# Routing by tiles, gate sums around the combination, and products of constants in two gaps of a hybrid decoder block

## The reference

```python
h = modulate(rms_norm(x, g_ffn[layer]), sh_f, sc_f)
g_logits = ht @ w_group + b_group
gate_group = softmax(g_logits)[g_sel]           # g_sel: the best group
e_logits = (ht @ w_erouter[g_sel]) + b_expert   # 8 experts of that group
top_vals, top_idx = lax.top_k(e_logits, 2)
top_w = jax.nn.softmax(top_vals, axis=-1)
...
out += (silu(ht @ w1[e]) * (ht @ w3[e]) * combine) @ w2[e]
x = x + gt_f * out
```

## Time and profile before

| | us |
|---|---|
| median of three runs | 626.9 |
| the profiled execution | 627.78 |
| its span | 625.8 |
| TensorE busy | 546.5 (87%) |
| VectorE busy | 294.6 (47%) |
| ScalarE busy | 184.0 (29%) |
| GpSimd busy | 79.0 (13%) |

### The profile page before, as it was taken

How to read it: one execution, slowest core, us unless ns; L and a number is a source line. 1 busy time by engine, 2 the same in 40 slices (tenths; PEclk the granted TensorE clock), 3 DMA queues, 4 the chain that set the end, 5 groups by cost and what they waited for, 6 DMA issues and landing times.

```text
span 625.8 us, 7694 instructions
## 1 busy us (share of the span) xinstructions
PE 546.5 (87%) x2982; PEld 343.9 (55%) x2982; DVE 294.6 (47%) x497; ACT 184.0 (29%) x328; POOL 79.0 (13%) x100
## 2 busy tenths in 40 slices
PE   1499999999978999999999747899999889879797
PEld 1377768778766676665446414445555444434443
DVE  4978673376798636562032284323322222312216
ACT  5265462344444457882042211000000000000002
POOL 8131100000010000000031111111221111110000
PEclk9999999999998999999999958999999999989999
DMA  8986855595262064001930485999999999999957
GB/s 336 398 262 232 308 193 205 172 366 202 68 214 90 2 264 206 1 1 51 426 128 34 186 339 177 407 417 421 422 420 419 419 421 420 421 420 420 410 233 293
DMA packets 42626, 169.28 MB, mean 271 GB/s; under 512 B 7848, under 2 KB 9896, under 8 KB 30308
## 3 DMA queue, kind: packets, MB, share of 16 engines
q1 hardware_dynamic: 32356, 140.81, 56.3%
q0 software_dynamic: 9104, 25.95, 11.8%
q10 hardware_dynamic: 1136, 2.11, 0.9%
HBM read 160.74 MB, written 16.25 MB: 283 GB/s over the span
## 4 chain that ended last, share of the span: by engine, by line
PE 61%; DVE 13%; DMA 13%; SPq 7%; ACT 4%; issue 2%; POOL 0%; DVEq 0%; ACTq 0%; POOLq 0%
PE banks L1784 11%; PE banks L1675 9%; PE banks L1804 5%; DMA qkT<-in_w_dram 5%; DMA obuf<-in_w_dram 4%; PE banks L1627 4%; PE banks L1510 4%; PE banks L1512 4%; PE banks L1511 4%; DVE mixT L893 3%; PE banks L1611 2%; DMA qkT<-in_w_ada_dram 2%; PE banks L1504 2%; PE banks L1502 2%; PE banks L1503 2%
## 5 line engine op out<-in xcount | busy, mean ns | idle before, releaser
L1804 PE MATMUL banks<-stage,work 128*64 128x512 f32 x168 | 60.1, 610 | 6.4 <-ACT work L855 6.4
L853 ACT ACTIVATE work<-banks 128x256 f32<-128x256 f32 x16 | 6.1, 383 | 200.3 <-PE banks L1784 200.3
L1784 PE MATMUL banks<-qkT,work 128*64 128x256 f32 x272 | 62.4, 386 | 0.0
L1675 PE MATMUL banks<-stage,mixT 128*128 128x512 f32 x128 | 56.2, 595 | 0.0
L1324 DVE TENSOR_TENSOR work<-banks,gates 128x1024 f32<-128x1024 f32 x15 | 18.4, 1225 | 74.5 <-PE banks L1804 74.5
L1318 DVE TENSOR_TENSOR work<-work,banks 128x256 f32<-128x256 f32 x16 | 6.7, 421 | 87.6 <-ACT work L853 87.6
L1784 PE MATMUL banks<-hT,work 128*64 128x256 f32 x192 | 44.0, 387 | 2.5 <-DMA qkT<-in_w_dram 2.5
L1512 PE MATMUL banks<-hT_hi,w_lo 128*128 128x512 f32 x112 | 43.8, 391 | 0.0
L893 DVE SCALAR_TENSOR_TENSOR mixT<-stage,small,mixT 128x1024 f32<-128x1024 f32 x32 | 41.0, 1282 | 0.7
L1510 PE MATMUL banks<-hT_hi,w_hi 128*128 128x512 f32 x96 | 40.4, 421 | 0.0
L1675 PEld LDWEIGHTS banks<-stage,mixT 128*128 128x128 f32 x128 | 24.1, 191 | 28.8 <-issue 28.8
(11 more groups left out here) (301 smaller groups left out, 1172.6 us busy)
## 6 DMA issues: line engine op xcount, KB each, us to landing
stage<-in_w_dram SPq DMA_DIRECT2D x31, 1024.0 KB
qkT<-in_w_dram SPq DMA_DIRECT2D x23, 1024.0 KB
stage<-in_w_ada_dram POOLq DMA_DIRECT2D x16, 1024.0 KB, 5.7
hT<-in_w_dram SPq DMA_DIRECT2D x12, 1024.0 KB
stage<-in_w_in_dram SPq DMA_DIRECT2D x5, 2048.0 KB, 11.0
val<-in_w_dram SPq DMA_DIRECT2D x10, 1024.0 KB
mixT<-in_w_dram SPq DMA_DIRECT2D x10, 1024.0 KB
alibi<-in_w_dram SPq DMA_DIRECT2D x5, 1024.0 KB
```

The costliest lines, as they stand in the source:

```text
L1675: ins = mm(banks[:, w % 5, :], mixT[:, k, t * P:(t + 1) * P], wv[:, k % 4, half * 512:(half + 1) * 512], start=(k == 0), stop=(k == KD - 1))
L1784: ins = mm(banks[half * C:(half + 1) * C, 2, up * F:(up + 1) * F], heT[:, r, k * P + half * C:k * P + (half + 1) * C], ws[2 * place + half ...
L1804: ins = mm(banks[half * C:(half + 1) * C, 4 + 2 * r + col, :], geT[:, fc * P + half * C:fc * P + (half + 1) * C], w2s[2 * place + half][:, ...
```

## The change

- `add_shift` waits for the tile's logits and for `r2_ready`, which ScalarE gives after the reciprocal root. ScalarE squares the last tile before it evicts x2T.
- The selection is put into functions on a range of tiles. Tiles 0 and 1 are done between the output halves 6 and 7, tile 2 around the copy of x2T, tile 3 after the last logits. The rank products are ordered by the tile they need. TensorE waits for `logits_read` before it writes logits of the tiles 2 and 3 into the bank that VectorE reads.
- Counts, column and slot are rounded by adding and subtracting 1.5 * 2^23 times the step. The table holds a key (1024 minus the token) and a second product of four passes says which choice it was; the rows to gather come from one instruction, the rows to scatter from two more. The scan for the plan moves behind the tables.
- `ADA_STEPS` goes from (0, 2, 4, 6, 8, 9, 10, 11) to (0, 2, 4, 6, 8, 10, 11, 12); from the fifth quarter on its first half stands before the combination, the second behind it and behind the splitting of weights. The first half of the second gate moves from step 12 to 13.
- Products of constants: 16 after the fourth and 12 after the seventh sum of the scale vector in the head, of 256 columns; 4 of 512 columns between the first two sets of transposes of experts' rows. TensorE waits for `scatter_ready` before the first of these.

```diff
-ADA_STEPS = (0, 2, 4, 6, 8, 9, 10, 11)
+ADA_STEPS = (0, 2, 4, 6, 8, 10, 11, 12)
+FILLERS_BETWEEN = 4
+HEAD_FILLERS = ((KD // 2, 16), (KD - 1, 12))
+TO_C, TO_P = 1.5 * 2.0 ** 23 * C, 1.5 * 2.0 ** 23 * P
...
-    steps[12].append((("gate", 1, 0), None))
+    steps[13].append((("gate", 1, 0), None))
...
             for t in range(NT):
+                act.wait_ge(x2_ready, 2 * t + 2)
+                a.activation(obuf[:, 2:4, :].rearrange("p a b -> p (a b)"), xr[:, t, :], ACT.Square,
+                             accum_out=ss2[:, t:t + 1]).then_inc(ss2_ready, 1)
                 if t == NT - 1:
...
-                link(a.activation(r2[:, t:t + 1], r2[:, t:t + 1], ACT.Exp, scale=-0.5))
+                a.activation(r2[:, t:t + 1], r2[:, t:t + 1], ACT.Exp, scale=-0.5).then_inc(r2_ready, 1)
+                act.wait_ge(r2_ready, t + 1)
...
                 if s in ADA_STEPS:
                     i = ADA_STEPS.index(s)
-                    ada_quarter(SCALE_F + i // 4, i % 4)
-                    if s < NT * DH:
-                        combine_unit(s)
+                    ada_open(SCALE_F + i // 4, i % 4)
+                    if i < 4:
+                        ada_close(SCALE_F + i // 4, i % 4)
+                    combine_unit(s)
...
                 for n in split_at(s):
                     w_rest(n)
+                if s in ADA_STEPS[4:]:
+                    i = ADA_STEPS.index(s)
+                    ada_close(SCALE_F + i // 4, i % 4)
...
+                if w == 2 * NT - 2:
+                    dve.wait_ge(memset_ready, 7)
+                    dve.wait_ge(logits_done, 2)
+                    link(v.tensor_copy(common, banks[:, 5, NT * NR:(NT + 1) * NR]))
+                    add_shift(0)
+                    add_shift(1).then_inc(logits_read, 1)
+                    dve.wait_ge(logits_read, 1)
+                    best_of_each(0, 2)
+                    second_of_each(0, 2)
+                    link(group_masks(0, 2))
...
+            add_shift(NT - 2).then_inc(logits_read, 1)
+            dve.wait_ge(logits_read, 2)
+            best_of_each(NT - 2, NT - 1)
             dve.wait_ge(fT_done, NT)
             dve.wait_ge(logits_done, NT - 2)
             v.tensor_copy(x2T[:, (NT - 1) % 2, 0:512], banks[:, 6, :]).then_inc(x2T_ready, 1)
+            second_of_each(NT - 2, NT - 1)
+            link(group_masks(NT - 2, NT - 1))
...
+            best_of_each(NT - 1, NT)
+            second_of_each(NT - 1, NT)
+            link(group_masks(NT - 1, NT))
+            link(v.memset(extra[:, 0:1], 0.0))
...
-            link(v.tensor_scalar(ints[:, 0:32], banks[:, 0, n32:n32 + 32], float(C - 1), None, ALU.add))
-            link(v.tensor_scalar(ints[:, 0:32], ints[:, 0:32], C.bit_length() - 1, None, ALU.arith_shift_right))
-            link(v.tensor_scalar(extra, ints[:, 0:32], -1.0, 0.0, ALU.add, ALU.max))
-            link(v.tensor_tensor_scan(incl, extra, zero32, 0.0, ALU.add, ALU.add))
-            link(v.tensor_tensor(obase, incl, extra, ALU.subtract))
-
-            link(v.scalar_tensor_tensor(out=obase, in0=obase, scalar=float(C), in1=over_base, op0=ALU.mult, op1=ALU.add))
+            link(v.tensor_scalar(extra[:, 1:E + 1], counts, -(C // 2 + 0.5), TO_C, ALU.add, ALU.add))
+            link(v.tensor_scalar(extra[:, 1:E + 1], extra[:, 1:E + 1], -TO_C, 0.0, ALU.add, ALU.max))
+            link(v.tensor_tensor_scan(obase, extra[:, 0:E], over_step, 0.0, ALU.add, ALU.add))
...
-            link(v.tensor_copy(posi, posf))
-            v.tensor_scalar(hi_i, posi, 4096 - P, None, ALU.bitwise_and)
-            link(v.tensor_scalar(lo_i, posi, P - 1, None, ALU.bitwise_and))
-            v.tensor_copy(rt[:, 1480:1488], lo_i)
-            link(v.tensor_copy(rt[:, 1488:1496], hi_i))
+            link(v.tensor_scalar(hi_big, posf, -(P // 2 - 0.5), TO_P, ALU.add, ALU.add))
+            link(v.scalar_tensor_tensor(out=lo_neg, in0=hi_big, scalar=TO_P, in1=posf, op0=ALU.subtract, op1=ALU.subtract))
...
-            link(v.tensor_scalar(free, held, 0.0, float(SKIP), ALU.is_equal, ALU.mult))
-            link(v.scalar_tensor_tensor(out=found, in0=held, scalar=-1.0, in1=free, op0=ALU.add, op1=ALU.add))
-            link(v.tensor_scalar(free, found, float(T), float(-T), ALU.is_ge, ALU.mult))
-            v.tensor_tensor(tables[:, 0, :], found, free, ALU.add).then_inc(table_ready, 1)
-            v.tensor_copy(tables[:, 1, :], found).then_inc(scatter_ready, 1)
+            v.tensor_scalar(tables[:, 0, :], held, -1.0, float(2 * T), ALU.mult, ALU.add).then_inc(table_ready, 1)
+            link(v.tensor_scalar(pair_row, held, -1.0, float(2 * T), ALU.mult, ALU.add))
+            v.scalar_tensor_tensor(out=tables[:, 1, :], in0=second_choice, scalar=float(T), in1=pair_row,
+                                   op0=ALU.mult, op1=ALU.add).then_inc(scatter_ready, 1)
...
+                    for rows_summed, count in HEAD_FILLERS:
+                        pe.wait_ge(scale_used, rows_summed)
+                        for n in range(count):
+                            mm(banks[:, 0, 256:512], ones_bf[:], ones_bf[:].unsqueeze(1).to_broadcast([P, 2, P]),
+                               start=False, stop=True, skip_group_check=True)
...
             logits(NT - 2)
             rows_T(NT - 1)
+            pe.wait_ge(y_scaled, 2 * NT)
+            pe.wait_ge(masks_ready, 1)
+            ranks_of(0)
+            ranks_of(1)
             logits(NT - 1)
+            pe.wait_ge(masks_ready, 2)
+            ranks_of(2)
+            pe.wait_ge(masks_ready, 3)
+            ranks_of(3).then_inc(rank_done, 1)
...
+            pe.wait_ge(scatter_ready, 1)
             expert_T(None, rows_of(0), 0)
+            for n in range(FILLERS_BETWEEN):
+                mm(banks[:, 7, :], ones_bf[:], ones_bf[:].unsqueeze(1).to_broadcast([P, NT, P]), start=True, stop=True)
             expert_T(None, rows_of(1), 1, 6)
```

More of the change, by code:

```diff
@@ L292, in hymba_block @@
             "xnb_ready", "xn_stored", "fT_done", "x2T_ready", "logits_done"))
+        ss2_ready, r2_ready, logits_read = sem("ss2_ready"), sem("r2_ready"), sem("logits_read")
         wrA_ready, x2T_act, scatter_ready = sem("wrA_ready"), sem("x2T_act"), sem("scatter_ready")
@@ L935, in ada_quarter, with ada_close @@
                 link(accumulate(acc[:, vec % 2, :], src[:, 0, :], 2 * i, i == 0))
+            def ada_close(vec, i):
+                n, src, _, _ = quarter(vec, i)
                 if i == 3 and vec in (SHIFT_F, SCALE_F):
@@ L1193, in _, with best_of_each @@
-            dve.wait_ge(logits_done, NT - 1)
-            link(v.tensor_copy(common, banks[:, 5, NT * NR:(NT + 1) * NR]))
-            dve.wait_ge(xnb_ready, NT - 1)
-            for t in range(NT - 1):
-                ins = add_shift(t)
-            link(ins)
+            def best_of_each(a, b):
+                r = slice(a * (G + 1), b * (G + 1))
+                n = (b - a) * (G + 1)
+                link(v.tensor_reduce(top1[:, r], lg[:, r, :], X, ALU.max))
+                link(v.tensor_tensor(first[:, r, :], lg[:, r, :], spread_rows(top1[:, r], n), ALU.is_equal))
+                link(v.tensor_tensor(first[:, r, :], first[:, r, :], rev.unsqueeze(1).to_broadcast([P, n, EG]), ALU.mult))
+                link(v.tensor_reduce(key1[:, r], first[:, r, :], X, ALU.max))
+                link(v.tensor_tensor(hot1[:, r, :], first[:, r, :], spread_rows(key1[:, r], n), ALU.is_equal))
@@ new lines, in second_of_each @@
+            def second_of_each(a, b):
+                r = slice(a * G, b * G)
+                n = (b - a) * G
+                link(v.scalar_tensor_tensor(out=rest.rearrange("p (t g) j -> p t (g j)", t=NT)[:, a:b, :],
+                                            in0=experts(hot1)[:, a:b, :], scalar=-1e30,
+                                            in1=experts(lg)[:, a:b, :], op0=ALU.mult, op1=ALU.add))
+                link(v.tensor_reduce(top2[:, r], rest[:, r, :], X, ALU.max))
+                link(v.tensor_tensor(second[:, r, :], rest[:, r, :], spread_rows(top2[:, r], n), ALU.is_equal))
+                link(v.tensor_tensor(second[:, r, :], second[:, r, :], rev.unsqueeze(1).to_broadcast([P, n, EG]), ALU.mult))
+                link(v.tensor_reduce(key2[:, r], second[:, r, :], X, ALU.max))
+                link(v.tensor_tensor(hot2[:, r, :], second[:, r, :], spread_rows(key2[:, r], n), ALU.is_equal))
@@ new lines, in of_group, with group_masks @@
+            def of_group(k, src, a, b):
+                return v.tensor_tensor(masks[:, k, a:b, :].rearrange("p t (g j) -> p t g j", g=G),
+                                       src[:, a:b, :].rearrange("p t (g j) -> p t g j", g=G),
+                                       gsel[:, a:b, :].unsqueeze(3).to_broadcast([P, b - a, G, EG]), ALU.mult)
+            def group_masks(a, b):
+                link(v.tensor_tensor(hots_t[:, a:b, :], hot2_t[:, a:b, :], experts(hot1)[:, a:b, :], ALU.add))
+                of_group(2, hots_t, a, b).then_inc(masks_ready, 1)
+                of_group(0, experts(hot1), a, b)
```

(25 more changed lines are left out.)

130 lines of the change are left out of this document (54 added, 76 removed).

## The result

The changed kernel takes **619.6 us** (median of 4, 618.37 to 620.81) against 626.28 for the kernel before on the same chip (4 runs): 0.9891 of it, with an interval of 0.9868 to 0.9914. It is faster by 6.7 us where 9.0 were forecast (617.9). The profiled execution took 618.37, its span is 616.4. The two spans shown, 625.8 and 616.4, lie 9.4 apart, but the first belongs to a slower execution of its kernel and the second to the fastest of its own. I go by the medians for what the change is worth, and by both pairs of traces for where it comes from.

The account below looks back on a forecast made before the run. The last 26 experts' weights were taken as a stream of fixed length (200 us) starting after the first `h1_done`. Head 0.9, gate sums 3.0 and routing 5.1 sum to 9.0: 626.9 - 9.0 = 617.9 us, range 615.4 to 622.2.

Parts of the forecast that it names:

- head: Scale vector's sums: 28 products of constants lift TensorE's clock, so ScalarE's evictions start sooner; 0.9 us, bound 1.0.
- gate sums: Attention steps 8 to 11: fewer VectorE sums ahead of the combinations shorten TensorE's waits; 3.0 us, ceiling 6.4.
- routing: From the last half of x2 to the first `h1_done`: earlier gather and kept clock bring it forward by 5.1 us.
- gather sooner: Routing: the table is ready 4.0 us sooner, so the gather starts 3.6 to 4.0 earlier; 3.8 taken.
- gather slowed by weights: The earlier gather meets weights still filling the DMA engines; 0 to 2 us lost, 0.7 taken, as gathered rows are few.
- clock kept between the transposes: First experts: four products hold TensorE at 2.4 GHz, turning rows 3.1 us earlier into `h1_done` 5.3 earlier, 5.1 taken.
- 9 sooner: Sign for the last experts' weight stream: its first weights issued and its last landing 9 us sooner.
- A: Rival: clock falls between the two transposes as before and the gather pays 2 us; 621.7 us, chance 0.16.
- B: Rival: attention gains 5.0 instead of 3.0, gather undisturbed, no doubt about the clock left; 615.0 us, chance 0.07.
- D: Rival: TensorE's waits in attention step 9 drop its clock to the end of step 12; 631.5 us, chance 0.03.
- C: Rival: routing and head leave nothing at the end, attention 2.0; 624.9 us, no measurable change, chance 0.05.
- E: Rival: rounding by addition gives another table, adding one expert pair to the stream; 633.2 us, chance 0.01.

Follow-up runs that it names:

- run 2: The kernel before with only the 28 products of constants in the head added: 625.02 us, ratio 0.9976 to the kernel before.
- run 1: The changed kernel without the 28 products of constants in the head: 621.94 us, ratio 0.9943 to the kernel before.
- run 3: The changed kernel with the gate sums as before (steps 8 to 11, both halves ahead of the combination): 622.47 us, ratio 0.9950 to the kernel before.
- run 5: The kernel before with head, gate sums and products between the transposes changed, but the old routing: 622.67 us, ratio 0.9942 to the kernel before.
- run 7: The changed kernel with w3 of the sixth expert issued only once the second gathered rows have landed: 616.57 us, ratio 0.9842 to the kernel before.
- run 4: The changed kernel without the four products of constants between the two sets of transposes: 619.87 us, ratio 0.9904 to the kernel before.
- run 6: The changed kernel and the kernel before, both unaltered, profiled again as the second pair of traces: 619.11 us and 626.77 us.
- run 10: The changed kernel with w3 of the sixth expert held back and without the four products between the transposes: 616.47 us, ratio 0.9840 to the kernel before.
- run 9: The kernel before with w3 of the sixth expert held back until the second gathered rows have landed: 625.62 us, ratio 0.9988.

## Why the prediction was nearly right, and where it failed

The time fell into the range (615.4 to 622.2), and the sign and the mechanism held: three gains add up to one earlier start of a stream of fixed length. The sum was 9.0 against 6.7 measured; the time missed by 1.7 only, since the sum was taken from 626.9 and the kernel before came to 626.28 beside the changed one. Term by term:

| term | counted | shown | by |
|---|---|---|---|
| head | 0.9 | 1.4 | run 2 and the trace of run 1; evictions 1.09 sooner |
| gate sums | 3.0 | 2.9 | run 3 |
| routing, of this: | 5.1 | 3.1 | run 5 |
| gather sooner | 3.8 | 4.4 | 20.5 to 16.1 after x2, in 12 of 13 traces |
| gather slowed by weights | -0.7 | -1.5 to -2.5 | 5.96 to 7.02, mean 6.4, against 4.51 to 4.67, mean 4.6; run 7 |
| clock kept between the transposes | 2.0 (2.2 less 0.2 for doubt) | about 0 | runs 4, 5, 6, 10 |

The three shown come to 7.4 by medians, within their errors of the 6.7. By the ratios to the kernel before, gate sums and routing would be 3.7 and 3.2, with an error of some 1.8 each; only the traces are finer than that. They give the routing less: from the last half of x2 to the first `h1_done` there are 31.7 to 32.4 in four traces of the old routing (33.8 in the one shown before), 29.1 to 31.4 in five of the new one, and 27.1 to 27.3 in the three with a weight held back. The means are 32.2, 30.2 and 27.2, so the routing gives 2.1, and 5.0 once its gather runs alone; with 1.4 and 2.8 the change comes to 6.3. Of the 3.0 between 30.2 and 27.2 the gather's rows are 2.1. Another 0.7 lies behind the first transposes: TensorE waits 1.8 to 2.7 for the late rows, and in three of the five traces its clock was down after that wait, in none of the three with a weight held back.

**Head: right**, a little more than its bound of 1.0. The bound followed ScalarE's evictions; TensorE's own transposes, which stand ahead of the projections, were at the lower clock too and gained the rest. All signs named for it were there, 1.95 for the sums of columns and 35.72 for the evictions (35.8 was forecast).

**Gate sums: right in size, and by its main argument**, that VectorE's work ahead of the combinations sets the time. The 1.6 that it added for the clock, "4.8 + 1.6 = 6.4", is not a second price: it is the wait that a faster TensorE has instead (run 2, 6.4 of waiting at the full clock). The waits for the combination are 2.6 and not under 2 as forecast, and there are the 1.3 for the bank, of which the prediction said that the product waits "as long as before". The time won is right all the same.

**Routing: two terms failed.** The first is "nearer to the first: 0.7", the delay of the gather by weights still moving. The argument was that the gathered rows are few. Few bytes didn't make it quick; what counted was how much of the weights the DMA engines still had to move. The gather paid 1.5 to 2.5, near or past the end of 2 that I kept for the range; with one weight held back it paid nothing (4.20), and the kernel gained 2.5. The Trainium skill (DMA: Bandwidth & Descriptors, Queues, rings and completion order) says that the DMA engines take their queues in turn, packet by packet, and by that the delay would have been near nothing. The runs don't agree with what the prediction made of that rule: neither the gather nor the store of 8.9 us came through as quickly as on idle queues. Whether the queues took turns can't be seen here, and why it didn't help was not tried.

The second is "5.3 at `h1_done`", the step from 3.1 for the rows to 5.3 for the first products, 2.2 in all, with 0.2 taken off for doubt. It compared the transposes at 1.84 and the expert products at 0.63 with a kernel in which the clock holds. In four other traces of the old routing, with and without the four products, the second transposes took 1.09 or 1.10 and the clock held anyway, in runs 2 and 9 after a pause of 1.22 and 1.36 like the 1.21 of the earlier trace rows. The price was read rightly from its rows, but they were those of one execution. In the new kernel the clock fell at the same place in one execution of two, with the four products there. Nor was the gap the place to guard: in the new kernel TensorE's longer wait stands ahead of the first transposes. The profiled execution was known to be 0.9 above the median; its low clock in the earlier trace rows was a place where that 0.9 could sit, and the sum took all of it for the kernel's. The same holds for another stretch that I did not price: from the sticks' first scores to the first exponential 11.42 us passed in that trace and 10.42 to 10.45 in every other one, with its first products at the lower clock:

```profile
232.47 0.80 PE L1627 MATMUL banks<-soft_hi,negtri 128*128 128x512 f32 x1
```

In the trace after, the same product:

```profile
228.21 0.51 PE L1664 MATMUL banks<-soft_hi,negtri 128*128 128x512 f32 x1
```

That 1.0, and the 1.4 to 2.1 by which its 33.8 above exceeds the other four, are most of what lies between the 9.4 of the two spans and the 6.7 of the medians. So the signs "9 sooner" at the start and the end of the stream came true (9.6 and 9.3) by the choice of the two executions, not by the sum: in the second pair both are 5.9 to 6.0 sooner. What the other traces give, 6.3, is inside the range too. But 619.6 lies even in the narrower one, 616.3 to 620, with a routing below its 3.9; the head above its 1.0 and a median before of 626.28, not 626.9, brought it there.

The table itself was counted well, from parts: selections on 32 elements take 0.19 instead of 0.29, and the last logits are added 6.8 behind the last half of x2 (352.77) or, at full clock, 6.0 (352.00, run 4). The fourth store didn't limit the gather: it landed 14.5 after the last half of x2 (360.50), the table was ready at 16.

**The rivals.** A (621.7) was nearest in mechanism, since its gather pays 2 us, but its other half, a clock that falls between the transposes, has no counterpart in four of five traces of the old routing. B's attention did not come: the 2.8 in the traces of run 3 leave no room for 5.0. D's wait ahead of the first product of step 9 did come, 1.3 us, but the product after it kept the clock (0.50, then 0.40), so its price was never paid. C (624.9) is excluded by the interval, and E by the length of the stream, 172.5 with no further pair.

## What to carry to other kernels

When a small transfer is made earlier, look at what the DMA engines are moving at its new time: here a gather of about 64 rows (1024 choices over 16 pairs) lost up to 2.5 us of a gain of 4.4 to a prefetch that nobody needed soon, and one wait moved ahead of the prefetch gave it back. Price a clock or a stall from more than one execution where the profiled one lies above the median, and treat its low-clock stretches as the first suspects for the excess. Products of constants are worth trying where TensorE is idle for several us ahead of a chain (1.4 us in the head), and not in a gap of 1.4 us or less (nothing in two pairs of runs). Price a lower clock only where TensorE sets the pace: in this attention it took 1.6 us out of a wait, and the time was the same.

## What the runs showed of the hardware that was not expected

- The granted clock of the profile reads 1.00 from 24 to 36 us in both kernels, but there 16 one-column products took 3.57, and 1.95 behind 28 products of constants (1.84 at the earlier trace rows). Durations told the level, the granted clock didn't.
- The same 16 products of 40 columns took 2.78 in one execution of the kernel after and 1.98 in another, four products of constants 1.03 and 1.91, and 16 products of w2 in the kernel before 3.65 and 5.27: the clock at a given place is not fixed by the program.
- A gather for whose data the weights had made room (DMA share 0.20 in the earlier trace rows, 0.32 in run 7) had its rows used 4.2 to 4.7 us behind its start; with the share at 0.80 to 1.05 meanwhile it was 5.96 to 7.02.
